# An expert stage fed from a pool of slots: another order of heavy and light passes, one slot more, and other ends of the stage

## The reference

```python
x = post_norm(x, concat([ya, yb, yc]) @ w_out[l], g_a, ln_g[l, 0], ln_b[l, 0])
h = x * (1.0 + sc_f) + sh_f
x = post_norm(x, moe_ffn(h, ...), g_f, ln_g[l, 1], ln_b[l, 1])

def moe_ffn(h, w_rg, w_re, w_g, w_u, w_d):
    pg = softmax(x @ w_rg)                       # 4 groups
    grp, g_w = argmax(pg), max(pg)
    le = (x @ w_re)[group grp]                   # 8 experts of that group
    top_l, top_i = top_k(le, 2)
    top_w = softmax(top_l) * g_w
    # the rows of each expert are gathered in blocks, and for each block
    out = (silu(xb @ w_g[e]) * (xb @ w_u[e])) @ w_d[e]    # 1024 -> 256 -> 1024
    y = sum over the row's two experts of out * top_w
```

## Time and profile before

| | us |
|---|---|
| median of 3 runs | 1575.5 (1571.06 to 1575.82) |
| profiled execution | 1570.34 |
| its span | 1568.5 |
| PE busy | 1417.3 (90%) |
| DVE busy | 605.1 (39%) |
| DMA, mean | 227 GB/s over the span |
| issues of expert weights `z<-in_w_exp` | 76, 1 MiB each, 22.5 us to landing |

### The profile page before, as it was taken

The page is one execution under the profiler, slowest core; times in us unless marked ns, Lnnn a source line. Parts: engine busy times, 40 slices in busy tenths (PEclk is TensorE's granted clock), DMA queues, the critical chain, the costliest instruction groups (busy, mean ns, idle before and its releaser), DMA issues.

```text
span 1568.5 us, 25207 instructions
## 1 busy us (share of the span) xinstructions
PE 1417.3 (90%) x9665; PEld 1085.2 (69%) x9665; DVE 605.1 (39%) x1445; ACT 335.2 (21%) x853; POOL 364.7 (23%) x467
## 2 busy tenths in 40 slices
PE   6999999898998999996899999989798889999664
PEld 4889889665887666553488989866577866656341
DVE  1121234678278122111352123357838832221106
ACT  2211211564111111100141121146511111111002
POOL 0100015632451211210010000654246231121101
PEclk9999999999998999998999999999999999999977
DMA  9310111774817999999532111257261589999954
GB/s 381 121 65 33 64 65 35 257 288 163 327 41 287 397 420 418 410 410 386 196 121 79 57 64 33 67 194 282 103 240 56 231 338 418 420 419 418 392 192 176
DMA packets 76741, 355.37 MB, mean 227 GB/s; under 512 B 20464, under 2 KB 23792, under 8 KB 43088
## 3 DMA queue, kind: packets, MB, share of 16 engines
q1 hardware_dynamic: 43632, 294.76, 47.5%
q0 software_dynamic: 19840, 44.63, 7.9%
q10 hardware_dynamic: 13152, 14.37, 2.8%
HBM read 341.25 MB, written 32.07 MB: 238 GB/s over the span
## 4 chain that ended last, share of the span: by engine, by line
PE 66%; SPq 10%; DMA 8%; DVE 7%; issue 4%; POOL 3%; ACT 1%; ACTq 0%; POOLq 0%; DVEq 0%
PE bank L1140 21%; PE bank L1497 10%; SPq L730 7%; PE bank L1519 5%; PE bank L1376 4%; PE bank L929 2%; PE bank L1124 2%; PE bank L832 2%; PE bank L1299 2%; DMA z<-in_w_exp 2%; DMA ring<-in_w_exp 2%; DMA att<-mod_rows 2%; PE bank L1273 1%; PE bank L1479 1%; PE bank L1086 1%
## 5 line engine op out<-in xcount | busy, mean ns | idle before, releaser
L1140 PE MATMUL bank<-ring,hT 128*128 128x256 f32 (+1 forms) x1600 | 339.2, 372 | 1.1 <-DVE z L2208 1.1
L1140 PEld LDWEIGHTS bank<-ring,hT 128*128 128x128 f32 x1600 | 291.8, 191 | 37.5 <-issue 1.6
L1497 PE MATMUL bank<-ring,att 128*64 128x256 f32 (+2 forms) x896 | 135.3, 421 | 27.6 <-DMA z<-in_w_exp 21.2
L1497 PE MATMUL bank<-z,att 128*64 128x256 f32 (+2 forms) x768 | 140.7, 405 | 10.8 <-DMA ring<-in_w_exp 7.4
L1376 PE MATMUL bank<-ring,hT 128*128 128x256 f32 x640 | 143.1, 383 | 1.7 <-ACT hT L1805 1.1
L1376 PEld LDWEIGHTS bank<-ring,hT 128*128 128x128 f32 x640 | 121.2, 192 | 17.9 <-issue 2.0
L2651 DVE TENSOR_TENSOR att<-att,bank 128x256 f32<-128x256 f32 x36 | 15.2, 421 | 298.0 <-ACT att L1893 298.0
L2986 POOL DMA_INDIRECT expert_rows<-att,cur x36 | 37.1, 1029 | 384.3 <-DVE att L2664 373.2
L1497 PEld LDWEIGHTS bank<-ring,att 128*64 128x64 f32 (+2 forms) x896 | 86.4, 149 | 54.9 <-DMA z<-in_w_exp 22.9
L1497 PEld LDWEIGHTS bank<-z,att 128*64 128x64 f32 (+2 forms) x768 | 90.7, 151 | 45.1 <-issue 12.7
L1519 PE MATMUL bank<-z,att 128*64 128x512 f32 (+2 forms) x224 | 79.8, 596 | 3.6 <-DVE att L2670 3.6
(11 more groups left out here) (401 smaller groups left out, 2331.3 us busy)
## 6 DMA issues: line engine op xcount, KB each, us to landing
z<-in_w_exp SPq DMA_DIRECT2D x76, 1024.0 KB, 22.5
ring<-in_w_exp SPq DMA_DIRECT2D x72, 1024.0 KB, 17.8
ring<-in_w_ada SPq DMA_DIRECT2D x41, 1024.0 KB, 5.9
ring<-in_w_in SPq DMA_DIRECT2D x24, 1024.0 KB, 5.0
hT<-in_w_exp SPq DMA_DIRECT2D x24, 1024.0 KB, 22.0
att<-in_w_exp SPq DMA_DIRECT2D x10, 1024.0 KB, 30.4
ring<-in_w_out SPq DMA_DIRECT2D x8, 1024.0 KB, 9.0
z<-expert_rows ACTq DMA_DIRECT2D x16, 512.0 KB, 8.6
```

The costliest lines, as they stand in the source:

```text
L1140: last = eng.matmul(bk[:, i * UN:i * UN + nw], hTv[:, k, t * P:(t + 1) * P], w[:, k, 0:nw], start=(k == 0), stop=(k == KD - 1))
L1497: last = eng.matmul(bank[2 + j][c * m_:(c + 1) * m_, u * DE:(u + 1) * DE], e["xT"][:, j, k * P + c * m_:k * P + (c + 1) * m_], wv[c][k // ...
```

## The change

The passes of a group go heavy, light, heavy, light, light. An 18th slot, the half of `att` that later holds the output rows, takes one piece, the last up of pass 1, which moves behind the four fixed downs. It isn't used again. SyncE's waits change with it: the twelfth piece waits for `h2` of two tiles, and `u` and `rows` are waited for at i=12; the others move on by one. The gate rows are loaded by GpSimd. VectorE does the weights and the gain before the counts; GpSimd adds the shifts before it waits for the late counts. TensorE releases the quad's gates and ups at later points, SyncE waits for the landed gates before the quad's downs, the quad may use the split slot, and a turn of the loop does `block_hT` before `block_x`.

```diff
-NSLOTS, SPLIT_SLOT, LATE_SLOT = 17, 15, 16
+NSLOTS, SPLIT_SLOT, LATE_SLOT, ONCE_SLOT = 18, 15, 16, 17
...
-    return "heavy" if b >= 2 and (b - 2) % 5 < 2 else "light"
+    return "heavy" if b >= 2 and (b - 2) % 5 in (0, 2) else "light"
...
-    return (2 * k + i,) if i < 2 else (NHEAVY + 6 * k + 2 * (i - 2), NHEAVY + 6 * k + 2 * (i - 2) + 1)
+    if i in (0, 2):
+        return (2 * k + i // 2,)
+    first = NHEAVY + 6 * k + 2 * (0, 0, 0, 1, 2)[i]
+    return first, first + 1
...
-    fixed = [(b, c, q) for b in range(2) for q in range(2) for c in range(2)] + [(b, c, 2) for b in range(2) for c in range(2)]
-    out = list(fixed)
+    gates_ups = [(b, c, q) for b in range(2) for q in range(2) for c in range(2)]
+    out = gates_ups[:-1] + [(b, c, 2) for b in range(2) for c in range(2)] + gates_ups[-1:]
...
-        free.append(n)
+        if n != ONCE_SLOT:
+            free.append(n)
...
-        wslot += [(region(hT, 4 * HALF, P, HALF), region(att, 7680, P, HALF)), region(z, 0, P, KD * UN)]
+        wslot += [(region(hT, 4 * HALF, P, HALF), region(att, 7680, P, HALF)), region(z, 0, P, KD * UN), region(att, 5632, P, KD * UN)]
...
-                                 + [12, 13, 6, 7, 11, 14, SPLIT_SLOT, LATE_SLOT])
+                                 + [12, 13, ONCE_SLOT, 6, 7, 11, 14, SPLIT_SLOT, LATE_SLOT])
...
@@ SyncE
-                eng.wait_ge(*ev.at("u", l, NT - 1))
-                eng.wait_ge(*ev.at("rows", l))
+                eng.wait_ge(*ev.at("h2", l, NT - 3))
+                eng.wait_ge(*ev.at("h2", l, NT - 1))
                 next_fixed(1)
...
-                    if i == 13:
+                    if i == 12:
+                        eng.wait_ge(*ev.at("u", l, NT - 1))
+                        eng.wait_ge(*ev.at("rows", l))
+                    elif i == 14:
                         eng.wait_ge(*ev.at("full", jobs.number(("RL", l, NT - 1))))
-                    elif i == 14:
+                    elif i == 15:
                         eng.wait_ge(*ev.at("w12", l))
...
-                done, count = after(last_late)
-                eng.wait_ge(W[done], count)
-                eng.wait_ge(*ev.at("st_modr", l))
-                for g in range(2):
-                    at = (g * 32 + 24) * P
-                    rows = mod_dram[l].rearrange("g a b -> (g a b)")[at:at + D].partition_broadcast(P)
-                    eng.dma_start(m["gf"][:, g, :], rows).then_inc(*sp.event(*(("ld_gf", l) if g else ("ld_gf", l, 0)), by=16, sem="ld_gf"))
...
                         eng.wait_ge(W[free], now(Count(i, 1, 1)))
+                        if q == 2:
+                            eng.wait_ge(W["quad_landed0"], now(Count(i, quad_total(l, 0), quad_total(l, 0))))
...
@@ TensorE
-                        if k == 0 and (b_ == PASSES - 1 or not isinstance(b_, int)):
-                            last.then_inc(W["quad_ups"], 1)
...
-                                if k == 0 and c == 0 and (b_ == PASSES - 2 and u == 0 or not isinstance(b_, int) and u == 1):
+                                if k == 0 and c == 0 and u == 1 and (b_ == PASSES - 2 or not isinstance(b_, int)):
                                     last.then_inc(W["quad_gates"], 1)
...
                         last = eng.transpose(bank[4][:, k * P:(k + 1) * P], e["hm"][:, parity(b_), k * P:(k + 1) * P], ident)
+                        if k == 0 and (b_ == PASSES - 2 or not isinstance(b_, int)):
+                            last.then_inc(W["quad_ups"], 1)
...
                 def turn(b_):
                     block_gates_ups(b_)
+                    block_hT(b_)
                     block_x(b_ + 1)
-                    block_hT(b_)
...
@@ VectorE
-                o1 = hot["past"]
+                eng.tensor_copy(hot["inc"], inc[0:1, :])
+                weights_of_two()
+                ln_gain(1, NT - 1, m["ln"], l)
+                o1, inc = hot["past"], hot["inc"]
...
-                weights_of_two()
-                ln_gain(1, NT - 1, m["ln"], l)
...
@@ GpSimd
-                    if b_ == 0:
-                        for t in range(NT - 2, NT):
-                            ln_shift(1, t, m["ln"], l)
...
+                    if b_ == PASSES - 2:
+                        done, count = after(POOL_OF[l][2])
+                        assert count <= PASSES - 1
+                        eng.wait_ge(W[done], count)
+                        for g in range(2):
+                            ld(m["gf"][:, g, :], mrow(g, 3), *(("ld_gf", l) if g else ("ld_gf", l, 0)))
...
                 gather(0)
                 gather(1)
+                for t in range(NT - 2, NT):
+                    ln_shift(1, t, m["ln"], l)
                 eng.wait_ge(*ev.at("ctl", l, "late"))
```

More of the change, by code:

```diff
@@ L523, in program @@
         r12 = {"e12": region(att, 8300 + NT * 36, P, 2 * NT, NE), "prod": region(att, 8300 + NT * 36 + 5 * NT * NE + 6 * NE, P, 2 * NT, NE)}
-        hot = layout(att, 3524, [("slot", P, 2 * NT, P), ("pass", P, 2 * NT, NLIST), ("past", 1, MAXOVF, NE), ("ctlf", 1, NCTL)])
+        hot = layout(att, 3524, [("slot", P, 2 * NT, P), ("pass", P, 2 * NT, NLIST), ("ctlf", 1, NCTL), ("inc", 1, NE)])
+        hot["past"] = region(att, 3524, 1, MAXOVF, NE)
         s5 = region(small, 0, P, 20, NT)
@@ L612, in entries, with quad_total @@
             return len(pass_experts(b_)) if isinstance(b_, int) and b_ < PASSES else QUAD
+        def quad_total(l, q):
+            return sum(32 if POOL_OF[l][0][(PASSES, c, q)][0] == SPLIT_SLOT else 16 for c in range(QUAD))
         def wait_landed(eng, l, b_, q):
             if not isinstance(b_, int):
-                eng.wait_ge(MOE[l][f"quad_landed{q}"], now(Count(b_.reg, 16 * QUAD, 16 * QUAD)))
+                eng.wait_ge(MOE[l][f"quad_landed{q}"], now(Count(b_.reg, quad_total(l, q), quad_total(l, q))))
                 return [POOL_OF[l][0][(PASSES, c, q)][0] for c in range(QUAD)]
@@ L720, in expert @@
                     return lambda q: A["w_exp"][l, bass.ds(ex, 1), q].rearrange("o p n -> p (o n)")
-                where, before, last_late = POOL_OF[l]
+                where, before, _ = POOL_OF[l]
                 def piece(b_, c, q, src):
                     n = where[(b_, c, q)][0]
+                    landed = slot_full[n] if b_ < PASSES else W[f"quad_landed{q}"]
                     if n == SPLIT_SLOT:
                         for half in range(2):
-                            eng.dma_start(slot_half(n, half), src(q)[:, half * HALF:(half + 1) * HALF]).then_inc(slot_full[n], 16)
+                            eng.dma_start(slot_half(n, half), src(q)[:, half * HALF:(half + 1) * HALF]).then_inc(landed, 16)
                         return
-                    eng.dma_start(wslot[n], src(q)).then_inc(slot_full[n] if b_ < PASSES else W[f"quad_landed{q}"], 16)
+                    eng.dma_start(wslot[n], src(q)).then_inc(landed, 16)
                 def fixed(n):
@@ L802, in _ @@
                 eng.wait_ge(*ev.at("x2", DEPTH - 1, NT - 1, half))
-                ld(y_rows(NT - 1)[:, cols], x[:, NT - 1, cols], "st_y", NT - 1, half)
+                eng.dma_start(y_rows(NT - 1)[:, cols], x[:, NT - 1, cols]).then_inc(*sp.event("st_y", NT - 1, half, by=16, sem="st_y_last"))
             for t in range(NT - 1):
                 eng.wait_ge(*ev.at("st_y", t))
-            for half in range(2):
-                eng.wait_ge(*ev.at("st_y", NT - 1, half))
+            eng.wait_ge(*ev.at("st_y", NT - 1, 1))
         @block.tensor
@@ L2682, in turn @@
                     hidden(b_)
+                    evac_hT(b_)
                     evac_x(b_ + 1)
-                    evac_hT(b_)
                     evac_out(b_)
```

## The result

The changed kernel takes 1582.35 us (median of 7 runs, 1580.35 to 1589.51) beside 1575.82 for the kernel before: a ratio of 1.0051 [1.0028, 1.0075]. Timed once more beside later variants it took 1581.63 us, 1.0043 [1.0026, 1.0060]. It is slower by about 7 us. The forecast was 1575.5.

A forecast was written before the change was run, and what follows sets the result against it. The expert stage was taken as bound by streamed weights on the DMA engines. Layer 0: -3.9 + 3.2 + 0.8 = +0.1; layer 1: -4.1 + 3.2 + 0.8 = -0.1; together 0.0, so 1575.5 us, range 1566 to 1582.

The forecast's parts named there:

- The bound and the empty time: Expert stage: set by streamed weights; DMA engines empty only early, 4.8 and 5.6 us, at most 10.4 us to fill.
- The cap: Piece 27 waits for pass 1's downs; backlog there 3.9 and 4.1 us, so gain at most 8.0, less any TensorE lateness.
- But the only place where the queue is nearly empty is before the downs of pass 1: Pass order step: both orders reach this place alike, afterwards the queue is full for 155 us, so 0.
- I take 3.2 us a layer: First gather of the stage: delayed 3.2 us a layer by earlier pieces, picked between +2.6 (half-met) and +3.9 (fully met).
- The upper bound (5.4): First gather: largest delay allowed, 10.1 - 4.7 = 5.4 us, from the worst gather into a full queue.
- Three pieces lie before it: First gather: three weight pieces ahead in the queue, given as the argument against the rival that the gather keeps its time.
- The estimate by the Trainium skill: First gather: would wait for about one piece's share, 2.5 us, layers gaining 0.7 us more each; not adopted.
- I take 0.8: TensorE's clock after idling about 3.6 us before pass 0: 0.8 us a layer, bounds 0 to 1.7.
- TensorE starts cold and late: Rival at the first gather and pass 0 gates: 7.1 us a layer against the caps, +6.2, 1581.7 us; chance 0.17.
- GpSimd's shifts, "nothing": Before the late counts: GpSimd's two shifts move ahead of a wait that is over by then, costing nothing.
- Pass order 0, gate rows 0, the wait before the last downs 0: New pass order, gate rows on GpSimd's queue, SP's wait for landed gates before the last four downs: each priced 0.
- the gate rows would burden the slower DMA engines: Rival at the stage's end: gate rows' 2.5 us come twice on a laggard, +5.0 us, 1580.5 us; chance 0.07.

The follow-up runs named there:

- changed, again: The changed kernel itself timed once more, nothing altered, beside later variants: 1.0043 of the kernel before, median 1581.63 us.
- changed, old pass order: The changed kernel with the passes in their old order (heavy, heavy, heavy, light, light): 1.0021 of the kernel before, 1580.02 us.
- changed, more fill: The changed kernel with 28 instead of 16 fill matmul sets ahead of the first transposes: 1.0025 of the kernel before, 1580.41 us.
- changed, shifts back: The changed kernel with GpSimd's two shift adds again behind its wait for the late counts: 1.0049 of the kernel before, 1583.10 us.
- gather first: The changed kernel with SyncE holding the att piece and what follows until the first gather has landed: 0.9999 of the kernel before, 1576.25 us.
- weights late: The changed kernel with VectorE's weights and gain again behind the overflow counts ("the late-weights version"): 0.9978 of the kernel before, 1572.02 us.
- weights late, downs at once: The changed kernel with VectorE's weights behind the counts and no wait for the last gates ahead of the last downs: 0.9975 of the kernel before, 1570.54 us.
- weights late, shifts back: The changed kernel with VectorE's weights and GpSimd's shifts both back behind the late counts: 0.9955 of the kernel before, 1569.15 us.
- other slots: The changed kernel with piece 27 on taking slots freed by pass 2's gates and ups before those of pass 1's downs: 0.9997 of before, 1577.12 us.

## Why the prediction was wrong

The ratios add up to a ledger of the change: 0.9997 for the rest of it, -0.42% for the 18th slot (0.9955), +0.23% for the shifts moved ahead (0.9978), +0.65% for the early weights (1.0043). The entries depend on the order in which they are taken: with the shifts back the early weights cost 0.94% (0.9955 to 1.0049), and the shifts then nothing that can be told. Step by step:

- **The bound and the empty time**: right. The stage is set by DMA time that stands empty early in it, and that time was 4.8 and 5.6 us. The 18th slot, a transfer of 2.5 us a layer, gives 1576.03 - 1569.15 = 6.9 us in the medians and 7.1 - 2.9 = 4.2 us in the stages; their uncertainty takes in the 5.0 us of two transfers.
- **The cap**: right in its mechanism. I had put the backlog at 3.9 and 4.1 us. TensorE was 7.5 and 6.3 us late at the downs of pass 1: 7.5 - 3.9 = 3.6 and 6.3 - 4.1 = 2.2 of loss; measured were 3.6 and 2.4. So near a hit is partly luck in a single profiled execution, but the same sum holds on both sides of the cap in the other kernels with 18 slots and the slots' old choice (late: the end of the downs of pass 1 behind the gather's issue, less 39.3 us):

| kernel | TensorE late (L0, L1) | less 3.9 and 4.1, both layers | stage |
|---|---|---|---|
| changed, again | 7.0, 6.8 | +5.8 | +6.0 |
| changed, old pass order | 6.8, 5.9 | +4.8 | +4.9 |
| changed, more fill | 4.8, 7.9 | +4.7 | +5.1 |
| changed, shifts back | 8.8, 7.0 | +7.8 | +7.9 |
| gather first | 2.3, 2.4 | -3.3 | -1.3 |
| weights late | 1.4, 1.5 | -5.1 | -4.6 |
| weights late, downs at once | 3.1, 1.5 | -3.5 | -3.0 |
| weights late, shifts back | 0.2, 0.1 | -7.8 | -7.1 |

  Gather first is off by 2.0 us, the others by 0.8 at most. The run with other slots takes away the wait and with it the rule: 8.4 and 7.9 us late, which would be +8.3, but +2.4.
- **"But the only place where the queue is nearly empty is before the downs of pass 1"**: wrong. Once TensorE is late, the gates of pass 0 stop the queue before that, and leave it empty for 5.2 and 3.6 us; I had not looked at the pieces that take their slots. It changes nothing in the sum, since piece 27 waits for the same late TensorE again, but it is what is left to lose with other slots.
- **"I take 3.2 us a layer"** for the gather: this is the term that failed. Measured were 9.95 - 4.72 = 5.2 and 8.65 - 4.70 = 3.9, mean 4.6. The upper bound (5.4) held. "Three pieces lie before it" was no reason for a loss: they are through within 1 us of the gather's issue, and the late-weights version has the same three and loses 1.0 and 0.0 us. The delay comes from the 2 MB behind it. I had picked between the two rows nearest in kind; the nearest in circumstance was the worst one of the earlier trace rows, 10.1 us, also a gather with pieces issued close to it. The estimate by the Trainium skill (DMA: Bandwidth & Descriptors, Queues, rings and completion order), one packet's turn or 2.5 us, was lower still; the measured 3.9 to 5.2 us decide against it as a price, and in layer 0 two pieces' worth (5.0) would be nearer.
- **"I take 0.8"** for the clock: the second one. Transposes 0.9 us and first gates 1.4 to 1.5 us longer, so 2.3 in each layer, more than the bound of 1.7, which left the transposes out and rested on gates alone.
- Both together are 7.5 and 6.3 us where I had 4.0. The sum 0.0 becomes +6.0. This is the rival "TensorE starts cold and late": 7.1 us a layer, +6.2, 1581.7 us. That it comes so near is in part luck: its gather bound was too high for layer 1 (5.4 against 3.9) and its clock bound too low (1.7 against 2.3). It had a chance of 0.17, though I had noted that it decides from 4.0 us on, my own estimate to the decimal: at that point a rival deserves about half. The time, 1582.35, is just above the range.
- **GpSimd's shifts, "nothing"**: wrong as a step, though without effect here. I asked what they waited for, not what they would run beside. The late counts ended at 511.75 instead of the 509.5 that I had given them, two small operations taking 1.79 and 2.12 us, and only the late gather hid it (VectorE, then GpSimd's two adds):

```profile
507.56 1.79 DVE L2637 TENSOR_SCALAR att<-att 1x40 f32<-1x40 f32 x1
509.28 0.14 DVE L2640 TENSOR_SCALAR att<-att 1x1 f32<-1x1 f32 x1
...
509.45 0.14 DVE L2642 TENSOR_SCALAR att<-att 1x1 f32<-1x1 f32 x1
509.63 2.12 DVE L2644 CAST att<-att 1x42 int32<-1x42 f32 x1
```
```profile
506.94 4.78 POOL L2921 TENSOR_TENSOR x<-x,z 128x1024 f32<-128x1024 f32 x2
```

- **Pass order 0, gate rows 0, the wait before the last downs 0**: right, each by a kernel of its own. That the gate rows would burden the slower DMA engines, the rival from the Trainium skill (same page, Latency and other measured facts), did not happen: 0.9994.
- What stays open: why pieces issued just behind a gather on another queue get ahead of it. The gather's issue ran 2.11 us in layer 0, but 1.10 in layer 1, where the gather still took 8.65 us, so a slow issue is not needed for the delay; whether the pieces get ahead while it is being issued, these runs don't show.

## What to carry to other kernels

Filling an idle queue pays only if nothing on the critical path has to pass through it: keep bulk transfers off for the few microseconds around a small transfer that an engine waits for. Here one slot more was worth 0.4%, and sending two pieces 3.5 us earlier cost the kernel before 0.61%. When work moves to an idle engine, read what runs beside it at its new place, and when two prices add up to a cap, forecast the side beyond the cap as often as the one within it.

## What the runs showed of the hardware

- The first gather of a stage, 128 rows, takes 4.2 to 5.7 us when no piece is issued until 3.5 us or more behind it, also with three 1 MB pieces issued 7 to 10 us ahead of it. It takes 7.8 to 11.0 us when 2 MB of pieces are issued on SyncE's queue from 0.1 us to between 1.1 and 1.9 us behind it (fourteen gathers, two in each of the seven versions with early weights and no hold).
- After 4.05 us of idling 8 transposes on TensorE took 1.97 us at a granted clock of 0.50, after 1.02 us of idling 1.09 us.
- VectorE operations of 0.17 to 0.29 us took 1.79, 2.12 and 2.74 us beside GpSimd's adds of 2.35 to 2.37 us, and ended within 0.04 us of the end of an add. A small VectorE operation can thus be held up by a whole one of GpSimd's. The Trainium skill says so (SBUF — State Buffer, SBUF: two separate sides): the port pair that both use is locked by one for a whole instruction; the trace agrees for VectorE. It does not fit in every detail: the lock is to go to the one that starts first, but the cast of 2.74 us began, by the records, 0.33 us ahead of the add. No run here shows the other direction, since GpSimd's second add waits for VectorE's multiplication on the same tile in any case. And not every small operation is stopped: that of 0.14 us at 509.28 ran about between the two adds, but one at 509.45, also of 0.14 us, ran beside the second.
